# Reading the kept activations and gates back from SyncE's queue instead of ScalarE's

## The chip, the core and the metric

The kernel runs on one core of a Trainium2 chip. The metric is the device time of one execution in microseconds (us). The engines of the core run their own instruction streams and meet only through semaphores: TensorE (PE in the profile, its weight loads PEld), VectorE (DVE), ScalarE (ACT), GpSimd (POOL) and SyncE (SP), which computes nothing and only issues DMAs. DMAs issued by SyncE, ScalarE and GpSimd run in three queues, q1, q10 and q0 of the profile, on the same 16 DMA engines.

## The reference

Two layers of a small transformer over 512 tokens of width 1024. Each layer is a hybrid mixer (attention and a gated recurrence), a layer norm, and a mixture of 16384 one-row experts (`peer_ffn`) whose top 16 per head are picked by product keys. The change lies in the last part:

```python
def block(xb):                       # 128 tokens
    ...                              # top 16 of 16384 experts for each of 8 heads: idx, gate
    act = jax.nn.gelu(jnp.einsum('thkd,td->thk', u[idx], xb).astype(jnp.float32), approximate=False)
    return jnp.einsum('thk,thkd->td', (gate * act).astype(xb.dtype), v[idx])
```

`u` and `v` are 16384 x 1024 in float32 for each layer.

## The kernel before

For the first 128 tokens the kernel gathers the chosen rows of `u` and `v` (GpSimd issues the gathers, VectorE does the sums). For the other 384 tokens it computes densely over all 16384 experts, in 128 tiles of 128 experts. The **first product** multiplies the tokens by every tile of `u`, applies gelu, and stores the activations to `act_dram`; the sparse gates are stored as a dense matrix to `gate_dram`. The **second product** multiplies gate times activation, called `w`, by every tile of `v`, and adds up over all 128 tiles in PSUM.

Every float32 operand is split into a high and a low part (`v_hi`, `v_lo`, `w_hi`, `w_lo`), and each product is three matmuls: high by low, low by high, high by high. For one tile `j` of the second product TensorE runs 6 x 3 = 18 matmuls of 512 columns (`matmul3`, L564), waits for `v_lo` and `w_lo` of that tile before it, and signals `y_done` behind it.

The work around it, with the order that each engine's program has:

- **SyncE** (L511 to L520) loads tile `j` of `v` into one of four places in `panel` as soon as the low part of tile `j - 4` is taken (`need_v_lo(pr, j - TILE_SLOTS)`). It loads nothing else in this stage but two gain vectors at `j == 8`.
- **ScalarE** (L1011 to L1022), in turn `j`: `split_v(j + 3)` (L956: waits for the landing of that tile and for `y_done` of j tiles, and writes `v_hi`), then `split_w(j + 2)` (L973: writes `w_hi`), and in every fourth turn, at `j = 6, 10, ... 114`, `fetch(j // 4 + 3)`: two DMAs (L960, L962) that read the activations and the gates of one panel of four tiles back, 768 KB each. Four panels (`WSLOTS`) have room. `fetch(0)` to `fetch(3)` are issued earlier, the last of them at `j == 2`.
- **VectorE** (L1617 to L1628), in turn `j`: when `j` is a multiple of 4, `weights(j // 4 + 1)` (L1584: activations times gates, waits for both landings); then `low_w(j + 2)` (L1590: waits for `w_hi` of that tile, writes `w_lo`); `low_v(j + 3)` if that is even (L1597: waits for `v_hi`, writes `v_lo`); then `add_row(j - 3)` (L1607, the gathered rows of the first 128 tokens).
- **GpSimd** (L1117 to L1121), in turn `j`: `v_lo` of tile `j + 3` if that is odd (L1111), then the gather of row `j + 3` (L1076, 512 KB).

All waits are in program order: an instruction behind a waiting one on the same engine waits too. A panel may be overwritten when `w_lo` of its four tiles is written, which is what the wait for `w_lo_ready` ahead of the fetch is for.

The loop of ScalarE:

```python
for j in range(NK):
    if j + URING < NK:
        split_v(j + URING)
    if j + 2 < NK:
        split_w(j + 2)
    ...
    if j % GROUP == 2 and j > 2 and j // GROUP + WSLOTS - 1 < UPANELS:
        act.wait_ge(w_lo_ready.sem, layer * w_lo_ready.per_layer + j // GROUP * GROUP)
        fetch(j // GROUP + WSLOTS - 1)
```

Of the kernel before, what the change touches and what calls it, by code (L numbers as in the profile page):

```python
# [23 lines left out]
GROUP = 4  # L24
UPANELS = NK // GROUP
# [12 lines left out]
WSLOTS = 4  # L38
# [24 lines left out]
def build(nc, x, pT, emb_g, emb_b, w_in, fox_fb, fox_g, lbl, hg_g, w_out, ln1_g, ln1_b,  # L63
# [5 lines left out]
    act_dram = nc.dram_tensor("act_scratch", (DEPTH, UPANELS, P, GROUP * DT), F32).ap()  # L69
    gate_dram = nc.dram_tensor("gate_scratch", (DEPTH, BLOCKS, P, NK, TB), F32).ap()  # L70
# [18 lines left out]
    with ExitStack() as ctx:  # L89
# [5 lines left out]
        def sig(name, per_layer, before=0):  # L95
            s = Signal(ctx.enter_context(nc.semaphore(name)), per_layer, before)
            names.append((name, s))
            return s
# [52 lines left out]
        def part(at, *shape):  # L151
            n = 1
            for s in shape:
                n *= s
            ap = arena[:, at:at + n]
            if len(shape) == 2:
                return ap.rearrange("p (a b) -> p a b", b=shape[1])
            if len(shape) == 3:
                return ap.rearrange("p (a b c) -> p a b c", b=shape[1], c=shape[2])
            return ap  # L160
# [36 lines left out]
        def wact(n):  # L197
            return part((20480, 0, 3072, 23552)[n % WSLOTS], GROUP, DT)

        def gin(n):  # L200
            return part((22016, 1536, 4608, 6144)[n % WSLOTS], BLOCKS, GROUP, TB)
# [28 lines left out]
        def u_tile(j):  # L230
            return panel[:, j % 4 // 2, j % 2 * D:(j % 2 + 1) * D]

        def v_tile(j):
            return panel[:, j % 4 // 2, j % 2 * D:(j % 2 + 1) * D]
# [112 lines left out]
        act_in = [sig(f"act_in{r}", 16 * UPANELS // WSLOTS) for r in range(WSLOTS)]  # L347
        gate_in = [sig(f"gate_in{r}", 16 * UPANELS // WSLOTS) for r in range(WSLOTS)]
# [5 lines left out]
        w_lo_ready = sig("w_lo_ready", NK)  # L354
# [50 lines left out]
        def need_v_lo(pr, j):  # L405

            pr.need(v_lo_odd if j % 2 else v_lo_even, j // 2 + 1)
# [38 lines left out]
        @block.sync  # L446
        def _(sp):
            sp.dma_start(h[:], x.rearrange("(i p) d -> p i d", p=P)).then_inc(x_in.sem, 16)
            sp.dma_start(lb_in[:], lbl).then_inc(lb_loaded.sem, 16)
            for k, a in enumerate((emb_g, emb_b)):  # L450
                sp.dma_start(lng[:, k, :], a.partition_broadcast(P)).then_inc(emb_in.sem, 16)
            sp.dma_start(cst[:], consts).then_inc(const_in.sem, 16)
            for layer in range(0, DEPTH):
                pr = Program(sp, layer)
                at = bass.ds(layer, 1)

                def load_panel(k):
                    dst = panel[:, k % 2]
                    if k == 0:

                        src = w_in[at, :, 3 * FW:3 * FW + P].rearrange("l (c p) n -> p (l c) n", p=P)
                        dst = dst[:, 0:NC * P].rearrange("p (c n) -> p c n", n=P)
                    elif k == K_PLE:
                        src = ple_w[at].rearrange("l (c p) n -> p (l c) n", p=P)
                        dst = dst.rearrange("p (c n) -> p c n", n=D)
                    else:
                        j, rows = ((k - 1) // 2, (k - 1) % 2) if k < K_U else ((k - K_GATE) // 2, (k - K_GATE) % 2)
                        w, col = (MIXER_PANELS if k < K_U else GATE_PANELS)[j]
                        src = w[at, rows * KC * P:(rows + 1) * KC * P, col:col + PANEL].rearrange(
                            "l (c p) n -> p (l c) n", p=P)  # L470
                        dst = dst.rearrange("p (c n) -> p c n", n=PANEL)
                    sp.dma_start(dst, src).then_inc(panel_in[k % 2].sem, 16)

                def row(a):
                    return a[at].rearrange("l d -> (l d)").partition_broadcast(P)


                if layer > 0:
                    sp.wait_ge(pled.sem, layer * pled.per_layer)
                    sp.wait_ge(v_lo_even.sem, layer * v_lo_even.per_layer)  # L480
                    sp.wait_ge(v_lo_odd.sem, layer * v_lo_odd.per_layer)
                load_panel(0)

                pr.mark(sp.dma_start(ff_bias[:], fox_fb[at].rearrange("l h -> h l")), ff_in, 16)
                load_panel(1)
                for k, a in enumerate((fox_g, hg_g)):
                    pr.mark(sp.dma_start(ng[:, k, :], row(a)), gains_in, 16)

                sp.wait_ge(h_ready.sem, layer * h_ready.per_layer + h_ready.before)
                for k, a in enumerate((ln1_g, ln1_b)):  # L490
                    pr.mark(sp.dma_start(lng[:, k, :], row(a)), ln1_in, 16)

                sp.wait_ge(dotted.sem, layer * dotted.per_layer)
                pr.mark(sp.dma_start(pTs[:], pT[at].rearrange("l (c p) t -> p (l c) t", p=P)), pT_in, 16)

                for k in range(2, K_PLE + 1):
                    if k == K_U - 6:
                        sp.wait_ge(h_ready.sem, layer * h_ready.per_layer + h_ready.before + NT)
                        pr.mark(sp.dma_start(keys_s, keysT[at].rearrange("l d a n -> d (l a) n")), keys_in, 16)
                    sp.wait_ge(ring_lo_ready.sem, layer * ring_lo_ready.per_layer + 2 + KC * (k - 2))  # L500
                    load_panel(k)

                for j in range(NK):
                    if j < 2:
                        sp.wait_ge(ring_lo_ready.sem, layer * ring_lo_ready.per_layer + SPLITS)
                    elif j < TILE_SLOTS:
                        sp.wait_ge(pled.sem, layer * pled.per_layer + 8)
                    else:
                        sp.wait_ge(u_lo_ready.sem, layer * u_lo_ready.per_layer + j - TILE_SLOTS + 1)
                    pr.mark(sp.dma_start(u_tile(j), u[layer, j]), u_in[j % TILE_SLOTS], 16)  # L510
                for j in range(NK):  # L511
                    if j == 2 * TILE_SLOTS:
                        sp.wait_ge(dotted.sem, layer * dotted.per_layer + SLOTS)
                        for k, a in enumerate((ln2_g, ln2_b)):
                            pr.mark(sp.dma_start(lng[:, k, :], row(a)), ln2_in, 16)
                    if j < TILE_SLOTS:
                        sp.wait_ge(u_lo_ready.sem, layer * u_lo_ready.per_layer + NK - TILE_SLOTS + j + 1)
                    else:
                        need_v_lo(pr, j - TILE_SLOTS)
                    pr.mark(sp.dma_start(v_tile(j), v[layer, j]), v_in[j % TILE_SLOTS], 16)  # L520


# [269 lines left out]
        def _(act):  # L792
# [5 lines left out]
            for layer in range(0, DEPTH):  # L798
                pr = Program(act, layer)
# [44 lines left out]
                for s in range(NS):  # L844
                    n = (s % NT + 1) * P
# [112 lines left out]
                def fetch(n):  # L958

                    pr.mark(act.dma_start(wact(n).rearrange("p g t -> p (g t)"), act_dram[layer, n]),  # L960
                            act_in[n % WSLOTS], 16)
                    pr.mark(act.dma_start(gin(n).rearrange("p j g t -> p j (g t)"),  # L962
                                          gate_dram[layer, :, :, n * GROUP:(n + 1) * GROUP, :]
                                          .rearrange("j p g t -> p j (g t)")), gate_in[n % WSLOTS], 16)
# [46 lines left out]
# [5 lines that stand above are left out]
                    if j == 2:  # L1016
                        act.wait_ge(dotted.sem, layer * dotted.per_layer + SLOTS)
                        pr.mark(nc.scalar.activation(wgt0, act0, ACT.Gelu), gelu0_done)
                        fetch(3)
                    if j % GROUP == 2 and j > 2 and j // GROUP + WSLOTS - 1 < UPANELS:  # L1020
                        act.wait_ge(w_lo_ready.sem, layer * w_lo_ready.per_layer + j // GROUP * GROUP)
                        fetch(j // GROUP + WSLOTS - 1)  # L1022
                root(4, rstd[:])


# [682 lines left out]
```

## Time and profile before

| | us |
|---|---|
| median of 3 runs | 3805.31 (3805.03 to 3805.52) |
| the profiled execution | 3803.14 |
| its span, first to last instruction | 3801.3 |
| TensorE busy | 3493.6 (92%) |
| VectorE busy | 2784.0 (73%) |
| GpSimd busy | 2183.2 (57%) |
| ScalarE busy | 1112.6 (29%) |
| the chain that ended last: matmuls of L564 | 61% of the span |

The second product of layer 0 starts at 1365.8 us of the span, and that of layer 1 ends at 3771.7 us. The stretches 1400 to 1800 us and 3300 to 3700 us lie wholly within the two. Where a group of instructions is busy for longer than the pitch at which its instructions follow each other, they overlap: a matmul of 512 columns is shown with 389 ns, and they start 0.226 us apart.

### The profile page before, as it was taken

How to read it: one execution, taken by the hardware profiler on the slowest of the kernel's cores; microseconds unless marked ns; L12 is line 12 of the kernel's file. 1: busy time of each engine (PE TensorE's matmuls, PEld its weight loads, DVE VectorE, ACT ScalarE, POOL GpSimd, SP SyncE). 2: the span in 40 equal slices, each digit the busy share in tenths (PEclk: the TensorE clock that was granted, in tenths of full speed). 3: DMA queues.
4: the chain of work that ended last, by engine and by line, in shares of the span. 5: the costliest groups of instructions: out<-in, count | busy, mean ns of one | idle time of the engine just before them, and what ended most of it. 6: DMA issues, size and time to landing. Idle time of an engine off the chain costs nothing.

```text
span 3801.3 us, 47667 instructions
## 1 busy us (share of the span) xinstructions
PE 3493.6 (92%) x17690; PEld 3065.9 (81%) x17690; DVE 2784.0 (73%) x5495; ACT 1112.6 (29%) x1748; POOL 2183.2 (57%) x1420
## 2 busy tenths in 40 slices
PE   6997779999989989999889977799999899899996
PEld 5766668899989978888777666679999899788885
DVE  5436636999896569999962374369988965899998
ACT  1112201334333333333221121013333333333332
POOL 5901467677646655555477025568666566555553
PEclk9956889999999999999999578899999999999998
DMA  4300022578868899999732001217888688999995
GB/s 138 98 14 1 12 78 79 187 261 311 295 232 298 301 380 357 353 352 354 258 94 89 1 1 34 78 67 242 275 295 300 229 312 305 370 354 356 353 354 184
DMA packets 316646, 822.01 MB, mean 216 GB/s; under 512 B 22400, under 2 KB 122752, under 8 KB 313088
## 3 DMA queue, kind: packets, MB, share of 16 engines
q1 hardware_dynamic: 112256, 349.15, 26.9%
q0 software_dynamic: 73728, 268.47, 19.1%
q10 hardware_dynamic: 130432, 201.34, 15.1%
q8 instruction: 142, 2.33, 0.2%
q14 instruction: 88, 0.72, 0.1%
HBM read 716.12 MB, written 102.76 MB: 215 GB/s over the span
## 4 chain that ended last, share of the span: by engine, by line
PE 74%; DVE 19%; POOL 2%; issue 2%; DMA 1%; ACT 1%; SPq 0%; ACTq 0%; DVEq 0%; POOLq 0%
PE ps L564 61%; PE ps L773 4%; PE ps L615 2%; DVE work L1467 2%; DVE state L1530 2%; PE ps L636 2%; PE ps L619 1%; DVE work L1471 1%; POOL ring_lo L1042 1%; DVE expert L1473 1%; DVE arena L1521 1%; DVE arena L1330 1%; PE ps L628 1%; POOL ring_hi L1040 1%; DVE arena L1338 1%
## 5 line engine op out<-in xcount | busy, mean ns | idle before, releaser
L1094 POOL TENSOR_TENSOR u_lo<-panel,u_hi 128x1024 fp32r<-128x1024 f32 x256 | 616.3, 2408 | 270.0 <-ACT u_hi L920 268.3
L564 PE MATMUL ps<-hT_hi,u_lo 128*128 128x384 f32 x2048 | 705.6, 345 | 3.9 <-POOL u_lo L1094 3.9
L564 PE MATMUL ps<-hT_lo,u_hi 128*128 128x384 f32 x2048 | 688.1, 336 | 0.0
L564 PE MATMUL ps<-hT_hi,u_hi 128*128 128x384 f32 x2048 | 687.8, 336 | 0.0
L564 PE MATMUL ps<-v_hi,w_lo 128*128 128x512 f32 x1536 | 599.8, 390 | 26.1 <-DVE w_lo L1590 26.1
L564 PE MATMUL ps<-v_lo,w_hi 128*128 128x512 f32 x1536 | 599.2, 390 | 0.0
L564 PE MATMUL ps<-v_hi,w_hi 128*128 128x512 f32 x1536 | 599.0, 390 | 0.0
L1111 POOL TENSOR_TENSOR v_lo<-panel,v_hi 128x1024 fp32r<-128x1024 f32 x128 | 348.5, 2723 | 389.7 <-ACT v_hi L956 381.3
L920 ACT CAST u_hi<-panel 128x1024 fp32r<-128x1024 f32 x256 | 268.1, 1048 | 723.1 <-PE ps L564 706.7
L956 ACT CAST v_hi<-panel 128x1024 fp32r<-128x1024 f32 x256 | 269.5, 1053 | 673.3 <-PE ps L564 665.6
L1590 DVE TENSOR_TENSOR w_lo<-arena,w_hi 128x384 fp32r<-128x384 f32 x256 | 393.9, 1540 | 93.8 <-ACT w_hi L973 93.7
L1040 POOL TENSOR_TENSOR ring_hi<-panel,cst 128x512 fp32r<-128x512 f32 x244 | 273.8, 1122 | 288.4 <-PE ps L564 174.8
L564 PEld LDWEIGHTS ps<-hT_hi,u_lo 128*128 128x128 f32 x2048 | 388.4, 190 | 5.4 <-POOL u_lo L1094 4.9
L564 PEld LDWEIGHTS ps<-hT_lo,u_hi 128*128 128x128 f32 x2048 | 388.1, 190 | 0.5 <-issue 0.5
L564 PEld LDWEIGHTS ps<-hT_hi,u_hi 128*128 128x128 f32 x2048 | 387.0, 189 | 0.0
L564 PEld LDWEIGHTS ps<-v_hi,w_lo 128*128 128x128 f32 x1536 | 289.4, 188 | 87.7 <-issue 27.3
L1042 POOL TENSOR_TENSOR ring_lo<-panel,ring_hi 128x512 fp32r<-128x512 f32 x244 | 336.3, 1378 | 19.1
L564 PEld LDWEIGHTS ps<-v_hi,w_hi 128*128 128x128 f32 x1536 | 289.3, 188 | 60.2
L564 PEld LDWEIGHTS ps<-v_lo,w_hi 128*128 128x128 f32 x1536 | 289.4, 188 | 60.0
L1607 DVE SCALAR_TENSOR_TENSOR ps<-rows_mem,arena,ps 128x1024 f32<-128x1024 f32 x256 | 327.2, 1278 | 0.4
L1067 POOL TENSOR_TENSOR arena<-arena 128x896 f32<-128x896 f32 x32 | 84.4, 2638 | 389.9 <-DVE arena L1338 389.9
L1076 POOL DMA_INDIRECT rows_mem<-in_v_rows,arena x256 | 264.6, 1033 | 58.3 <-issue 44.8
(220 smaller groups left out, 6284.2 us busy)
## 6 DMA issues: line engine op xcount, KB each, us to landing
panel<-in_u SPq DMA_DIRECT2D x256, 512.0 KB, 4.2
panel<-in_v SPq DMA_DIRECT2D x256, 512.0 KB, 6.8
act_scratch<-arena ACTq DMA_DIRECT2D x128, 384.0 KB, 4.1
gate_scratch<-arena ACTq DMA_DIRECT2D x24, 2048.0 KB, 9.3
arena<-act_scratch ACTq DMA_DIRECT2D x64, 768.0 KB, 6.7
arena<-gate_scratch ACTq DMA_DIRECT2D x64, 768.0 KB, 14.3
panel<-in_w_in SPq DMA_DIRECT2D x28, 1024.0 KB, 5.2
panel<-in_wq SPq DMA_DIRECT2D x16, 1024.0 KB, 5.1
```

What stands on the lines that cost most here:

```text
L564: mm = nc.tensor.matmul(o, lhs[a], rhs[b_], start=(start and n == 0), stop=(stop and n == 2))
L773: mm = nc.tensor.matmul(g_bank(k)[:, c * NK:(c + 1) * NK], hot1[:, k % 2, c, :], hot2[:, k % 2, c, :], start=True, stop=True)
L920: pr.mark(nc.scalar.copy(u_hi[:, j % URING].rearrange("p c n -> p (c n)"), u_tile(j)), u_hi_ready)
L956: pr.mark(nc.scalar.copy(v_hi[:, j % VRING], v_tile(j)), v_hi_ready)
L1040: nc.gpsimd.tensor_tensor(r_hi[:, at], src, zeros, ALU.subtract).then_inc(ring_hi_ready.sem, 1)
L1042: nc.gpsimd.tensor_tensor(r_lo[:, at], src, r_hi[:, at].bitcast(F32), ALU.subtract).then_inc(ring_lo_ready.sem, 1)
L1067: pr.mark(nc.gpsimd.tensor_tensor(ke, ke, kT[:, hd:hd + 1, i * P:(i + 1) * P].to_broadcast([P, LEVELS - 1, P]), ALU.mult), lev_mul)
L1076: pr.mark(nc.gpsimd.indirect_dma_start(out=dst, out_offset=None, in_=rows, in_offset=bass.IndirectOffsetOnAxis(ap=idx0[:, s:s + 1], axis=0 ...
L1094: pr.mark(nc.gpsimd.tensor_tensor(u_lo[:, j % URING].rearrange("p c n -> p (c n)"), u_tile(j), u_hi[:, j % URING].rearrange("p c n -> p (c ...
L1111: pr.mark(nc.gpsimd.tensor_tensor(v_lo[:, j % VRING], v_tile(j), v_hi[:, j % VRING].bitcast(F32), ALU.subtract), v_lo_odd)
L1590: pr.mark(nc.vector.tensor_tensor(w_lo[:, j % GROUP], wact(j // GROUP)[:, j % GROUP], w_hi[:, j % GROUP].bitcast(F32), ALU.subtract), w_lo ...
L1607: pr.mark(nc.vector.scalar_tensor_tensor(out=acc0, in0=v_rows_in[s % VBUF], scalar=wgt0[:, s:s + 1], in1=acc0, op0=ALU.mult, op1=ALU.add), ...
```

## The change

The fetches at `j = 6, 10, ... 114` are taken out of ScalarE's program and put into SyncE's loop over the tiles of `v`. At the same `j` numbers, with the same wait for `w_lo_ready`, SyncE issues the two DMAs of the panel directly ahead of the load of tile `j`. The `j` of the two loops is not the same moment: SyncE's `j` is the tile that it loads, ScalarE's `j` the turn in which it splits tile `j + 3`. `fetch(0)` to `fetch(3)` stay where they were.

```diff
@@ SyncE, loop over the tiles of v @@
                     else:
                         need_v_lo(pr, j - TILE_SLOTS)
+                    if j % GROUP == 2 and j > 2 and j // GROUP + WSLOTS - 1 < UPANELS:
+                        n = j // GROUP + WSLOTS - 1
+                        sp.wait_ge(w_lo_ready.sem, layer * w_lo_ready.per_layer + j // GROUP * GROUP)
+                        pr.mark(sp.dma_start(wact(n).rearrange("p g t -> p (g t)"), act_dram[layer, n]),
+                                act_in[n % WSLOTS], 16)
+                        pr.mark(sp.dma_start(gin(n).rearrange("p j g t -> p j (g t)"),
+                                             gate_dram[layer, :, :, n * GROUP:(n + 1) * GROUP, :]
+                                             .rearrange("j p g t -> p j (g t)")), gate_in[n % WSLOTS], 16)
                     pr.mark(sp.dma_start(v_tile(j), v[layer, j]), v_in[j % TILE_SLOTS], 16)
@@ ScalarE, loop of the second product @@
-                    if j % GROUP == 2 and j > 2 and j // GROUP + WSLOTS - 1 < UPANELS:
-                        act.wait_ge(w_lo_ready.sem, layer * w_lo_ready.per_layer + j // GROUP * GROUP)
-                        fetch(j // GROUP + WSLOTS - 1)
```

SyncE's queue at the start of the second product, with - as it was and + as it is now (`in_v` is a tile of `v`, `act_scratch` and `gate_scratch` the kept activations and gates):

```order
 L510 DMA panel<-in_u 128x1024 x128
-L520 DMA panel<-in_v 128x1024 x8
+L528 DMA panel<-in_v 128x1024 x6
+L523 DMA arena<-act_scratch 128x1536
+L525 DMA arena<-gate_scratch 128x12x128
+L528 DMA panel<-in_v 128x1024 x2
 L515 DMA lng<-in_ln_g 128x1024
 L515 DMA lng<-in_ln_b 128x1024
-L520 DMA panel<-in_v 128x1024 x120
+L528 DMA panel<-in_v 128x1024 x2
+L523 DMA arena<-act_scratch 128x1536
+L525 DMA arena<-gate_scratch 128x12x128
```

Ahead of tile 6, and of every fourth tile behind it up to 114, there are now two more DMAs; before, nothing but tiles stood in this queue.

ScalarE before, in the turns behind `fetch(3)` (`CAST v_hi` is `split_v`, `CAST w_hi` is `split_w`); this piece repeats every four turns:

```order
L956 CAST v_hi<-panel 128x1024
L973 CAST w_hi<-arena 128x384
L960 DMA arena<-act_scratch 128x1536
L962 DMA arena<-gate_scratch 128x12x128
L956 CAST v_hi<-panel 128x1024
L973 CAST w_hi<-arena 128x384
```

Now the two DMAs between the splits are gone, and the splits follow each other in the same order as before. The programs of TensorE, VectorE and GpSimd are the same.

## Rows read from the trace of the kernel before

**Rows 1.** Busy time by stretch (windows): engines, PEclk, DMA share, GB/s; both layers.

```profile
1500.00:1600.00 100.00, 100.00 (x443) 82.81 (x442) 91.64 (x68) 35.95 (x50) 58.91 (x37) 1.00 1.00 354
...
sum 800.00, PE 800.00 PEld 662.40 DVE 733.29 ACT 286.98 POOL 470.19; mean PE 100.00 PEld 82.80 DVE 91.66 ACT 35.87 POOL 58.77
```

**Rows 2.** Waits, 1400 to 1800 us: us in total, times, longest.

```profile
ACT v_hi L956 <- PE ps L564: 253.5, 97, 2.9
...
DVE w_lo L1590 <- ACT w_hi L973: 32.5, 47, 1.0
...
ACT v_hi L956 <- DMA panel<-in_v: 2.9, 1, 2.9
```

**Rows 3.** Waits of SyncE's queue in the same stretch.

```profile
SPq L520 <- POOL v_lo L1111: 208.2, 49, 4.8
SPq L520 <- DVE v_lo L1597: 157.1, 49, 4.5
```

**Rows 4.** Timeline of ScalarE: start, duration, work; one fetch and the splits behind.

```profile
1507.61 0.33 ACTq L960 DMA_DIRECT2D arena<-act_scratch  x1
1507.96 0.46 ACTq L962 DMA_DIRECT2D arena<-gate_scratch  x1
...
1511.58 1.05 ACT L956 CAST v_hi<-panel 128x1024 fp32r<-128x1024 f32 x1 [2.62 <-PE ps L564]
1512.54 0.50 ACT L973 CAST w_hi<-arena 128x384 fp32r<-128x384 f32 x1
```

**Rows 5.** Timeline of VectorE, from `low_w` of tile 4m+1 to that of 4m+3.

```profile
1513.08 0.56 DVE L1590 TENSOR_TENSOR w_lo<-arena,w_hi 128x384 fp32r<-128x384 f32 x1 [0.44 <-ACT w_hi L973]
1513.56 1.22 DVE L1597 TENSOR_TENSOR v_lo<-panel,v_hi 128x1024 fp32r<-128x1024 f32 x1
1514.69 1.28 DVE L1607 SCALAR_TENSOR_TENSOR ps<-rows_mem,arena,ps 128x1024 f32<-128x1024 f32 x1
1515.88 1.75 DVE L1584 TENSOR_TENSOR arena<-arena 128x1536 f32<-128x1536 f32 x1
1517.55 2.75 DVE L1590 TENSOR_TENSOR w_lo<-arena,w_hi 128x384 fp32r<-128x384 f32 x1
1520.23 1.28 DVE L1607 SCALAR_TENSOR_TENSOR ps<-rows_mem,arena,ps 128x1024 f32<-128x1024 f32 x1
1521.42 0.61 DVE L1590 TENSOR_TENSOR w_lo<-arena,w_hi 128x384 fp32r<-128x384 f32 x1
```

**Rows 6.** Timeline of GpSimd beside it: two gathers, and the next odd `v_lo`.

```profile
1511.17 1.09 POOL L1076 DMA_INDIRECT rows_mem<-in_v_rows,arena  x1
1512.57 0.94 POOL L1076 DMA_INDIRECT rows_mem<-in_v_rows,arena  x1 [0.30 <-issue]
1516.80 3.09 POOL L1111 TENSOR_TENSOR v_lo<-panel,v_hi 128x1024 fp32r<-128x1024 f32 x1 [3.28 <-ACT v_hi L956]
```

**Rows 7.** DMA, 1400 to 1800 us: queues (packets, MB, share); issues (us to landing).

```profile
q1 hardware_dynamic: 14349, 52.29, 36.4%
q0 software_dynamic: 14112, 51.39, 33.8%
q10 hardware_dynamic: 41617, 38.22, 29.7%
...
panel<-in_v SPq DMA_DIRECT2D x98, 512.0 KB, 6.8
arena<-act_scratch ACTq DMA_DIRECT2D x24, 768.0 KB, 6.6
arena<-gate_scratch ACTq DMA_DIRECT2D x24, 768.0 KB, 14.2
rows_mem<-in_v_rows,arena POOLq DMA_INDIRECT x99, 7.5
```

**Rows 8.** The tile `panel` in that stretch: landings of single tiles.

```profile
DMA to landing us min/median/max: 3.5/6.8/9.4
```

**Rows 9.** Timeline of TensorE: the first matmul of the second product, layer 0.

```profile
1365.83 0.77 PE L564 MATMUL ps<-v_hi,w_lo 128*128 128x512 f32 x1 [11.67 <-DVE w_lo L1590]
```

**Rows 10.** Window behind it: TensorE alone, then PEclk, DMA share, GB/s.

```profile
1370.00:1374.00 4.00, 4.00 (x19) 1.00 1.03 400
```

## The prediction

> **What bounds the kernel now.** I read the busy time by stretch first, to find out which engine is full in the stage that the change touches. In 800 us taken from the two second products TensorE is busy for all 800, at a granted clock of 1.00, and the DMA engines' share is 1.00 too [rows 1]. So TensorE sets the time here, with 443 matmuls in 100 us: 18 x 100 / 443 = 4.06 us for a tile, 16.25 us for a panel of four. VectorE is next with 91.7%, ScalarE far behind with 35.9%.
>
> Then the waits, to see what is late. ScalarE's `split_v` waits for TensorE in 97 of 98 turns, 253.5 us of 400, and once in 400 us for a tile of `v` to land, 2.9 us [rows 2]. SyncE waits 365 us of 400, always for the low part of a tile, thus for a free place [rows 3]. No row of TensorE is among the waits of this stretch. The reader is to see from this that tiles of `v` are early, that nothing can be gained in the steady part (a full TensorE can't be fuller), and that the question is only whether the change makes something late.
>
> **What it removes.** ScalarE issues two DMAs less for each panel, 0.33 + 0.46 us [rows 4], 28 times in each layer. ScalarE waits for TensorE during most of its time [rows 2], so this is worth 0.
>
> **What it adds.** SyncE issues them. Its time for that, 0.79 us of 16.25, fits its waiting [rows 3]. The panels arrive earlier, which helps nobody: VectorE's `weights` waits for no landing in the steady part, its only wait there is for `w_hi` [rows 2]. Two other things are added to the way of tile 4m+2 of `v`, which now stands behind the fetch. First, SyncE waits until `w_lo` of tile 4m-1 is written. Second, 1.57 MB stand ahead of the tile in the same queue.
>
> **First look: is the tile still in time?** I follow one panel. `w_lo` of tile 4m-1 is the last of rows 5, written at 1521.42 + 0.61 = 1522.03. `split_v` of tile 4m+2 is the row at 1511.58 [rows 4], thus due again at 1511.58 + 16.25 = 1527.83. From the release to the due time there are 5.8 us. Call the time from release to landing Λ.
>
> The trace has no tile behind a fetch in one queue, so I bound Λ. A tile by itself lands after 3.5 us at the least [rows 8]. The fetch ahead of it takes the DMA engines, at the best rate that a stretch shows, 400 GB/s [rows 10], 1.573 / 0.400 = 3.9 us; by the share of its queue, 29.7% of 400 us for 24 pairs [rows 7], 4.9 us. The row gathers of GpSimd's queue run between: 33.8% of 400 us for 99 rows, 1.4 us each, or 1.3 at 400 GB/s. With none of them in the way Λ is 3.5 + 3.9 = 7.4 to 8.4 us. With two of them it is 7.4 + 2.6 = 10.0 to 8.4 + 2.8 = 11.2. Far above these there is another row: gates land 14.2 us after their issue now [rows 7], and with the issue ahead, 0.35, and a tile behind, 1.5 (36.4% of 400 us for 98 tiles), that makes 16.1. I take two gathers and the middle, 10.6, because GpSimd issues its gathers in pairs behind an odd `v_lo` [rows 6] and such a pair is in flight at that moment (worked out below). I don't take 16.1, since today the gates share the engines with tiles of a second queue, which would now stand behind them.
>
> So every value of Λ is above 5.8, and the tile comes late, by 4.8 us with my value. TensorE bears about 3.5 us of this: `w_lo` of tile 4m+2 is written at 1517.55 + 2.75 = 1520.30 [rows 5], and needed three tiles after 1511.58, at 1523.8.
>
> **Second look: the lateness feeds itself.** ScalarE's order is `split_v(4m+2)`, then `split_w(4m+1)`, then VectorE's `low_w(4m+1)`. The w row starts 1513.08 - 1511.58 = 1.5 us behind the start of the v split [rows 4, 5]. From there VectorE works without a gap through seven instructions to the end of `low_w(4m+3)`, 1522.03 - 1513.08 = 8.95 us [rows 5]. That end is the release of the **next** fetch, behind which the next tile 4m+6 stands. So there is now a closed ring of work: tile lands, 1.5 + 8.95 = 10.45 us, release, Λ, next tile lands. It must go round once in four tiles, and it takes 10.45 + 10.6 = 21.05 us, where TensorE needs 16.25. TensorE gets 4.8 us idle in each panel.
>
> Bounds of the first part: one of the seven, the `w_lo` of 2.75 us, is stretched while GpSimd's `v_lo` runs beside it (1516.80, 3.09 us [rows 6]); the same operation takes 0.56 and 0.61 in the other rows [rows 5]. If the late timing moves the two apart, 10.45 becomes 8.3. I keep 10.45, because in the ring an odd tile lands right behind the even one, and GpSimd again works while VectorE does these seven. On the pair of gathers: with the tile landing at 0, TensorE starts tile 4m+1 at 2.1 and ends it at 6.1, then `v_hi` of the next odd tile (1.05), `v_lo` on GpSimd (2.4 to 3.1), and the gathers at about 10 and 11.4 [rows 4, 6], beside a release at 10.45. Both are in Λ.
>
> **The sum.** 28 fetches in each layer, two layers: 56 x 4.8 = 269 us. The first of each layer has no ring behind it, but comes when the DMA engines are over-full (share 1.03 [rows 10]); I count it like the others. Profiled execution 3803.14 + 269 = 4072, and the median of the runs lies 2 us above that execution: **4070 us**. TensorE's granted clock may fall after its new gaps, as it was low for the first matmul behind an idle time of 11.67 us (0.77 us [rows 9] against 0.39); I add nothing, since TensorE isn't in the ring.
>
> **A rule against this reading.** The traces show act data landing after 6.6 us and gates of the same size, issued 0.35 us later in the same queue, after 14.2, while tiles in another queue land in 6.8 [rows 7]: it matters what stands ahead in one's own queue. The Trainium skill, "DMA: Bandwidth & Descriptors", section "Issuing engines are not separate DMA queues", says that DMAs of all issuing engines run on the same 16 DMA engines and interleave, and that the choice of the issuing engine saves only sequencer time; read by itself this gives a change worth nothing. The same page's section "Queues, rings and completion order" says that each DMA engine goes round between queues and takes the descriptors of one queue in their order; by that the tile waits for the whole fetch.
>
> **Rivals.**
>
> 1. *The ring is short enough (not slower).* Place: the landing of tile 4m+2. If Λ is at most 16.25 - 8.3 = 8.0 us together with the short VectorE part, the ring fits under TensorE and the cost is 0: 3803 to 3805 us. For it: the low ends, 7.4 and 8.3, sum to 15.7. Against it: both must hold at once, with no gather in the way, when the DMA share is 1.00 [rows 1]. This is also what the rule on issuing engines would give. Chance 0.05.
> 2. *A small ring*, 16.4 to 18 us, when the gathers miss the fetch or GpSimd misses VectorE: 56 x up to 1.75 = up to 98 us, 3810 to 3900. Chance 0.06.
> 3. *The gates hold the tile for as long as they take now*, Λ = 16.1: 10.45 + 16.1 = 26.5, 56 x 10.3 = 577 us, 4380. For it: 14.2 is measured. Against it: while TensorE idles, the same 16 us of DMA work are spread over 21 and more. Chance of anything above 4180: 0.07.
> 4. *Faster.* ScalarE's queue is free at the start of the stage. But TensorE is busy for 4.00 of 4.00 us right behind its start [rows 10], and its idle 11.67 us [rows 9] wait for `fetch(0)` and its `w`, which aren't moved. Chance 0.02.
> 5. *The change doesn't do what it says*: the order of SyncE's queue shows that it does. 0.
>
> **How the numbers follow.** The ring at 18 to 23 us has 0.80. 18 us give 3803 + 98 = 3900; 23 us, my value with 2 us more for the slowest of the 16 DMA engines, give 3803 + 378 = 4180. The range is 3900 to 4180; what is left out is 0.20. A measurement of this kernel can tell about 0.2% from no change, 8 us. Faster 0.02, within 0.05, slower 0.93 (0.80 + 0.06 + 0.07).
>
> **What would show it.** In the changed kernel's windows of the second product: TensorE busy near 16.25 / 21 = 77%, VectorE near 71%, DMA share below 0.9. In the waits: `split_v` waits for the landing of `panel` about once in each panel, and TensorE for `w_lo`. In SyncE's waits: one for `w_lo` of L1590 in each panel. The fetches are about 21 us apart. Wrong would be: fetches 16.3 us apart with TensorE at 100% (rival 1), or TensorE's waits on something that is not behind tile 4m+2. The first product must be as it was.

## The result: 4199.9 us against 3805.4, slower by 10.4%

The changed kernel takes 4199.89 us (median of 4 executions, 4195.92 to 4208.58), the kernel before, beside it, 3805.41 us. The ratio is 1.104 with a 95% interval of 1.102 to 1.106. The forecast was 4070 with a range of 3900 to 4180: the direction and the mechanism came out, the size did not, and the time lies above the range.

The profile after: its span is 4206.7 us. The windows of the second product of layer 0, five of them from 1400 to 1900 us, with the columns of rows 1:

```profile
1500.00:1600.00 100.00, 79.88 (x309) 63.85 (x308) 55.47 (x46) 22.84 (x32) 45.40 (x27) 0.86 0.70 246
1600.00:1700.00 100.00, 77.59 (x305) 61.45 (x303) 53.59 (x44) 22.88 (x33) 42.43 (x24) 0.88 0.72 256
...
sum 500.00, PE 399.11 PEld 318.06 DVE 288.29 ACT 122.56 POOL 232.85; mean PE 79.82 PEld 63.61 DVE 57.66 ACT 24.51 POOL 46.57
```

TensorE fell from 100 to 80%, with 305 matmuls in 100 us instead of 443 [rows 1], and the DMA engines from 1.00 to 0.70. Nothing is full any more: VectorE has 58% and the DMA engines 70%. When every engine gets emptier and the time grows, the work has been put in a row that was side by side.

The waits between 1500 and 1900 us, and below them those of SyncE's queue, answer rows 2 and 3:

```profile
ACT v_hi L964 <- DMA panel<-in_v: 232.8, 23, 17.0
...
DVE w_lo L1595 <- ACT w_hi L981: 171.5, 17, 12.7
...
PE ps L572 <- DVE w_lo L1595: 81.4, 19, 7.4
ACT v_hi L964 <- PE ps L572: 68.5, 17, 5.5
```

```profile
SPq L522 <- DVE w_lo L1595: 277.0, 17, 18.0
```

`split_v` waited 253.5 us for TensorE and 2.9 for a tile [rows 2]; now it waits 68.5 us for TensorE and 232.8 for tiles. SyncE waited only for free places [rows 3]; now it waits for `w_lo`, 17 times, once for each panel, 16.3 us each.

The chain of waits in the stretch 1620 to 1650 us (start, duration, what) goes once round the ring:

```profile
1617.89 11.08 DMA panel<-in_v
...
1629.94 0.52 ACT w_hi L981
...
1630.96 1.22 DVE v_lo L1602
1632.18 0.92 DVE ps L1612
...
1636.64 0.55 DVE w_lo L1595
1637.19 1.20 DVE ps L1612
1638.39 3.26 DVE w_lo L1595
...
1641.71 0.33 SPq L523
...
1642.08 0.61 SPq L525
...
1642.74 11.00 DMA panel<-in_v
```

There is no TensorE in it. A tile lands, ScalarE and VectorE work from `w_hi` of tile 4m+1 to `w_lo` of tile 4m+3, SyncE issues the fetch, and the next tile lands 11 us behind its own issue. The page's section on the whole chain says the same in shares:

```profile
PE 45%; DVE 24%; DMA 18%; issue 7%; POOL 2%; ACT 2%; SPq 1%; ACTq 0%; DVEq 0%; POOLq 0%
PE ps L572 34%; DMA panel<-in_v 17%; PE ps L781 4%; DVE ps L1612 3%; PE ps L623 2%; DVE work L1472 2%; DVE w_lo L1595 2%; DVE state L1535 2%; PE ps L644 1%; DVE v_lo L1602 1%; DVE work L1476 1%; PE ps L627 1%; POOL ring_lo L1047 1%; DVE expert L1478 1%; DVE arena L1526 1%
```

The fetches are 23.6 us apart (the mean of the 54 intervals in both layers, from the issues in SyncE's timeline; the first of each layer is 29.7 or 29.8 us, the others are 23.4 in the mean), instead of 16.3. 56 x (23.6 - 16.3) = 409 us; the spans differ by 405.

Of two fetches that follow each other, here is SyncE's timeline, and what it issues behind them:

```profile
1617.05 0.33 SPq L523 DMA_DIRECT2D arena<-act_scratch  x1
1617.41 0.44 SPq L525 DMA_DIRECT2D arena<-gate_scratch  x1
1617.89 5.78 SPq L528 DMA_DIRECT2D panel<-in_v  x4
1641.71 0.33 SPq L523 DMA_DIRECT2D arena<-act_scratch  x1
```

And ScalarE's, at the landing between them:

```profile
1628.99 1.04 ACT L964 CAST v_hi<-panel 128x1024 fp32r<-128x1024 f32 x1 [10.32 <-DMA panel<-in_v]
1629.94 0.51 ACT L981 CAST w_hi<-arena 128x384 fp32r<-128x384 f32 x1
```

From the issue at 1617.05 to the landing at 1628.99 are 11.9 us, one of the shortest of the ring's DMA parts; over the 56 fetches the mean is 14.0 us, from 11.9 to 17.5. The other part, landing to next issue, is 9.6 us in the mean, and here, at 12.7, one of the longest.

### The profile page after: what moved, and what is told of

Read it like the earlier page. It is cut to its first block, busy times and chain, and to the rows that moved or that the text cites. A ratio compares the mean times of both kernels' runs of the same rounds, so it can differ in the third digit from the quotient of the medians.

```text
span 4206.7 us, 47723 instructions
## 1 busy us (share of the span) xinstructions
PE 3621.3 (86%) x17690; PEld 3139.9 (75%) x17690; DVE 2687.2 (64%) x5495; ACT 1103.9 (26%) x1748; POOL 2250.1 (53%) x1420
## 4 chain that ended last, share of the span: by engine, by line
PE 45%; DVE 24%; DMA 18%; issue 7%; POOL 2%; ACT 2%; SPq 1%; ACTq 0%; DVEq 0%; POOLq 0%
PE ps L572 34%; DMA panel<-in_v 17%; PE ps L781 4%; DVE ps L1612 3%; PE ps L623 2%; DVE work L1472 2%; DVE w_lo L1595 2%; DVE state L1535 2%; PE ps L644 1%; DVE v_lo L1602 1%; DVE work L1476 1%; PE ps L627 1%; POOL ring_lo L1047 1%; DVE expert L1478 1%; DVE arena L1526 1%
## 5 line engine op out<-in xcount | busy, mean ns | idle before, releaser
L572 PE MATMUL ps<-v_hi,w_lo 128*128 128x512 f32 x1536 | 654.9, 426 | 299.3 <-DVE w_lo L1595 298.8
L572 PE MATMUL ps<-v_lo,w_hi 128*128 128x512 f32 x1536 | 641.9, 418 | 0.0
L572 PE MATMUL ps<-v_hi,w_hi 128*128 128x512 f32 x1536 | 639.0, 416 | 0.0
L572 PEld LDWEIGHTS ps<-v_hi,w_lo 128*128 128x128 f32 x1536 | 318.3, 207 | 395.6 <-issue 326.4
L1595 DVE TENSOR_TENSOR w_lo<-arena,w_hi 128x384 fp32r<-128x384 f32 x256 | 221.5, 866 | 598.7 <-ACT w_hi L981 598.6
L572 PEld LDWEIGHTS ps<-v_hi,w_hi 128*128 128x128 f32 x1536 | 314.8, 205 | 71.7
L572 PEld LDWEIGHTS ps<-v_lo,w_hi 128*128 128x128 f32 x1536 | 318.1, 207 | 67.1
L1081 POOL DMA_INDIRECT rows_mem<-in_v_rows,arena x256 | 332.3, 1298 | 66.6 <-issue 42.2
```

Source lines behind the costliest of these rows:

```text
L572: mm = nc.tensor.matmul(o, lhs[a], rhs[b_], start=(start and n == 0), stop=(stop and n == 2))
L1081: pr.mark(nc.gpsimd.indirect_dma_start(out=dst, out_offset=None, in_=rows, in_offset=bass.IndirectOffsetOnAxis(ap=idx0[:, s:s + 1], axis=0 ...
L1595: pr.mark(nc.vector.tensor_tensor(w_lo[:, j % GROUP], wact(j // GROUP)[:, j % GROUP], w_hi[:, j % GROUP].bitcast(F32), ALU.subtract), w_lo ...
```

## Experiments

The text behind "expected" was written before each run. There are 14 kernels. The kernel before, run beside them, had a median of 3803.8 us (kernels e1 to e4), 3804.5 (e5, e6, e7, e9) and 3805.7 (e8, e10 to e12), and in one execution beside the last two 3814.6. Where no ratio is given, there is one execution of the kernel; e3, e9 and f1 leave out 120 of the 128 gathers of `v` in each layer, and f2 the gates that it doesn't read. I call **Λ** the time from the end of `low_w` of tile 4m+3 to the landing of the next tile 4m+2 (the start of its `split_v`, which waited for it), and **D** the time from there to the end of the next such `low_w`; both are read from the timelines of VectorE and ScalarE between 1500 and 1900 us, 16 to 20 panels each. Where no view shows the landing of a single tile, it is read from the updates of that tile's semaphore in the trace.

| kernel | us | Λ | D | ring |
|---|---|---|---|---|
| changed | 4199.9 | 13.6 | 9.7 | 23.3 |
| wait alone | 4051.2 | 9.6 | 11.5 | 21.1 |
| activations only | 4074.2 | 11.1 | 10.3 | 21.3 |
| changed, long pieces | 4127.2 | 12.6 | 9.7 | 22.2 |
| changed, no gathers | 4018.6 | 9.7 | 10.1 | 19.8 |

### e1: the wait alone

```diff
# kernel before, SyncE's loop; the fetches stay on ScalarE
+ if j % GROUP == 2 and j > 2 and j // GROUP + WSLOTS - 1 < UPANELS:
+     sp.wait_ge(w_lo_ready.sem, layer * w_lo_ready.per_layer + j // GROUP * GROUP)
  pr.mark(sp.dma_start(v_tile(j), v[layer, j]), v_in[j % TILE_SLOTS], 16)
```

> The fetches stay on ScalarE as in the kernel before; SyncE only gets the wait for w_lo of tile 4m-1 ahead of tile 4m+2. Ring theory: the ring is closed, 9.5 us (tile landed to release, as the changed kernel shows) plus the landing of a tile that stands behind nothing, 3.5 to 6.8 us, so 13 to 16.3 us in all, against 16.25 us of TensorE: 0 to 50 us over the kernel before, 3805 to 3855. Rival, the wait alone is the cause (the tile comes too late whatever stands ahead of it): about the whole loss, 4150 to 4200.

Measured: 4051.24 us, ratio 1.0655 (1.0633 to 1.0678). Neither text had it right. The wait alone makes 247 of the 395 us, with not one byte added to SyncE's queue. Its windows and SyncE's waits:

```profile
1600.00:1700.00 100.00, 85.31 (x344) 66.99 (x343) 68.95 (x52) 26.07 (x37) 46.47 (x28) 0.95 0.79 286
```

```profile
SPq L521 <- DVE w_lo L1592: 329.1, 19, 19.9
```

The ring is there with 21.1 us. I had expected 3.5 to 6.8 us for a tile with nothing ahead in its queue; it is 9.6. The other queues' work stands around the release: in this trace ScalarE issues a fetch 1.3 to 5.0 us ahead of the held tile, and GpSimd a gather 3.7 to 3.9 us and another 0.3 or 1.1 us ahead of it (1500 to 1900 us). That the gathers lengthen Λ is shown by e9 below; the part of this fetch in it was not taken apart.

### e2: the bytes without the wait

```diff
# changed kernel, SyncE's loop: the same fetch, one panel later in the program
- if j % GROUP == 2 and j > 2 and j // GROUP + WSLOTS - 1 < UPANELS:
-     n = j // GROUP + WSLOTS - 1
-     sp.wait_ge(w_lo_ready.sem, layer * w_lo_ready.per_layer + j // GROUP * GROUP)
+ if j % GROUP == 2 and j // GROUP > 1 and j // GROUP + WSLOTS - 2 < UPANELS:
+     n = j // GROUP + WSLOTS - 2
+     sp.wait_ge(w_lo_ready.sem, layer * w_lo_ready.per_layer + (j // GROUP - 1) * GROUP)
```

> The fetches stand ahead of tiles 4m+2 in SyncE's queue as in the changed kernel, but each one panel later in the program (ahead of tile 4m+6 instead of 4m+2), so its wait for w_lo is long fulfilled: the bytes ahead of the tile without the wait. Ring theory: the only ring left goes through v_lo of the tile four before, 3.2 us plus 12 to 14 us to the landing, 15.2 to 17.2 us against 16.25: 0 to 55 us over the kernel before, 3805 to 3860. Rival, the 1.57 MB ahead in the same queue are the cause by themselves: the loss stays mostly, 4100 to 4200.

Measured: 3810.78 us, ratio 1.0017 (1.0007 to 1.0027), near the low end of the ring theory's text, and far from the rival's 4100 to 4200. The same 1.57 MB stand ahead of every tile 4m+2, and cost 7 us in all. SyncE's timeline shows the pace of TensorE, and the tile `panel` the landings of all tiles, 11.3 us behind the issue at the most:

```profile
1602.53 0.33 SPq L523 DMA_DIRECT2D arena<-act_scratch  x1
1602.90 0.43 SPq L525 DMA_DIRECT2D arena<-gate_scratch  x1
1603.38 12.34 SPq L528 DMA_DIRECT2D panel<-in_v  x4
1618.85 0.33 SPq L523 DMA_DIRECT2D arena<-act_scratch  x1
```

```profile
DMA to landing us min/median/max: 3.5/7.5/11.3
```

So the bytes ahead of the tile are not a cause by themselves. They lengthen a ring, and cost time only where one is closed. From the issue of the fetch to the landing of tile 4m+2 are 10.7 us here in the mean (10.0 to 12.1 between 1500 and 1875 us), where the changed kernel has 13.5 in the same stretch.

### e3: what is in Λ, the gathers

```diff
# changed kernel, GpSimd: only the first 8 gathers of v; VectorE waits only for those
+ if s < VBUF:
      gather(v_rows, v_rows_in[s % VBUF], s, v_row_in[s % VBUF])
```

> The changed kernel without 120 of the 128 row gathers of v in each layer (the sums over the gathered rows then use old rows; this part of the computation is left out). It measures what the gathers have in the 14 us from release to landing. Ring theory with three to four gathers of 1.3 to 1.4 us in them: 14 falls to 8.5 to 10, the ring to 18 to 19.5 us, 3900 to 3990. If the prediction's two gathers were right and something else is slow: 11 to 11.5 us, ring near 20.7, 4050. If the gathers have no part in it: 14 us stay, 4190.

Measured: 4018.57 us. Λ falls from 13.6 to 9.7, by 3.9 us, which is nearly three gathers of 1.4 us [rows 7]. Λ hit the first text, the time missed it by 29 us, since D is 10.1 and not 9.5. The prediction had two gathers in it. The removal also takes their issue out of GpSimd's program, so 3.9 us is what the gathers do in all, and not the DMA time of three of them by measurement.

### e5 and f2: what is in Λ, the fetch, half of it, and its pieces

```diff
# changed kernel: the gates go back to ScalarE at j % 4 == 2, the activations stay on SyncE
- pr.mark(sp.dma_start(gin(n)..., gate_dram[layer, :, :, n * GROUP:(n + 1) * GROUP, :]...), gate_in[n % WSLOTS], 16)
+ pr.mark(act.dma_start(gin(n)..., gate_dram[layer, :, :, n * GROUP:(n + 1) * GROUP, :]...), gate_in[n % WSLOTS], 16)
```

> As the changed kernel, but only the activations (0.79 MB) are read back on SyncE's queue, ahead of tile 4m+2 and behind the wait; the gates stay on ScalarE at their old place. If bytes ahead of the tile lengthen the ring in proportion, half of the step from the wait alone (4051) to the whole change (4200) is left: 4110 to 4150. If the gates with their 1536 pieces of 512 B are the slow part: 4050 to 4080. If any fetch ahead of the tile costs the same: 4180 to 4200.

Measured: 4074.24 us, one execution. Λ is 1.5 us above that of the wait alone, D 1.2 us below. All three kernels read the same bytes; what differs is the queue in which they stand. A byte is not a byte here, since the gates, as many, add 2.5 us more when they too go ahead of the tile.

```diff
# changed kernel: the second DMA of the fetch reads 768 KB in rows of 6 KB
- gate_dram[layer, :, :, n * GROUP:(n + 1) * GROUP, :].rearrange("j p g t -> p j (g t)")
+ act_dram[layer, n]
```

> The changed kernel, but the second DMA of each fetch on SyncE's queue reads the 768 KB of the activations once more instead of the gates: the same bytes at the same place of the queue, without the source's pieces of 512 B (the product of gate and activation is thus not computed there). Measured so far: act alone ahead of the tile adds 1.5 us to the landing, act and gates 4.6. If a byte is a byte: 14.2 us stay within 0.7, 4170 to 4200. If the pieces of 512 B are dear: 14.2 falls to 12.6, twice the step of the activations, 4100 to 4130.

Measured: 4127.23 us. Λ is 12.6, 1.0 us less with the same bytes. So of the gates' 2.5 us some 1.0 is due to their pieces of 512 B, and 1.5 to their bytes, as with the activations.

### e4: the tile first

```diff
# changed kernel, SyncE's loop at j % 4 == 2
  sp.wait_ge(w_lo_ready.sem, layer * w_lo_ready.per_layer + j // GROUP * GROUP)
+ pr.mark(sp.dma_start(v_tile(j), v[layer, j]), v_in[j % TILE_SLOTS], 16)
  pr.mark(sp.dma_start(wact(n)..., act_dram[layer, n]), act_in[n % WSLOTS], 16)
  pr.mark(sp.dma_start(gin(n)..., gate_dram[...]), gate_in[n % WSLOTS], 16)
- pr.mark(sp.dma_start(v_tile(j), v[layer, j]), v_in[j % TILE_SLOTS], 16)
```

> The changed kernel with tile 4m+2 issued directly ahead of the fetch instead of behind it; the wait stays ahead of both. Ring theory: tile 4m+2 now lands 4 to 7 us behind the release, and the ring goes through tile 4m+3, which stands behind the fetch: from its landing 1.5 us to w_hi, then low_w(4m+2), add_row, low_w(4m+3), 2.3 to 4.6 us, then 12 to 14 us to the next landing, 16 to 20 us, middle 18: 3805 to 4015, middle 3905. Rival, all bytes of the queue count wherever they stand: no change, 4190.

Measured: 4128.15 us. A gain of 72 us over the changed kernel, far less than expected: tile 4m+2 lands 7.9 us behind the release (mean of the panels between 1500 and 1900 us), but the release itself waits longer, since tile 4m+3 is now the late one and `low_w(4m+2)` and `low_w(4m+3)` need it. The ring has 22.1 us. To order the queue otherwise gave back only 72 of the 395 us while all of it stood behind one release.

### e6: one instruction earlier

```diff
# kernel with the wait alone
- sp.wait_ge(w_lo_ready.sem, layer * w_lo_ready.per_layer + j // GROUP * GROUP)
+ sp.wait_ge(w_lo_ready.sem, layer * w_lo_ready.per_layer + j // GROUP * GROUP - 1)
```

> As the kernel with the wait alone (fetches on ScalarE), but SyncE waits for w_lo of tile 4m-2 instead of 4m-1, one instruction of each kind earlier in VectorE's program. Ring theory: the VectorE part of the ring gets 1.75 us shorter (add_row and low_w), so the ring of 20.7 us goes to about 19, 3803 + 56 x 2.7 = 3950, 3930 to 3970. If the mere presence of a wait ahead of the tile costs (not when it is fulfilled): 4050 as with the full wait. If there is a threshold in the timing and not a ring: 3805.

Measured: 3801.62 us. Waiting for `w_lo` of tile 4m-2 instead of 4m-1 takes away the whole loss. SyncE still waits for `w_lo` once a panel:

```profile
SPq L521 <- DVE w_lo L1592: 178.7, 20, 8.9
SPq L522 <- POOL v_lo L1113: 98.8, 25, 4.8
```

but its rings no longer set the pace: the tiles 4m+2 from 14 to 114 of layer 0 land 3.5 to 6.4 us behind their issue, 3.8 in the median, and at least 1.2 us before `split_v` takes them.

The time fits the third text, the one against the ring. The ring can still be added up, but only with a Λ from this kernel: from the landing to the end of `low_w(4m+2)` are 1520.30 - 1511.58 = 8.7 us [rows 4, 5], and 8.7 + 3.8 = 12.5 us, 15.1 with the largest, is less than 16.3. My 19 us were wrong because I took Λ over from the slow kernel. The one instruction of each kind by itself doesn't close the ring either: 10.45 + 3.8 = 14.3 us. Λ must grow as well, and it does, as the first held tile of e10 below shows: 7.5 us. What differs around the two issues is GpSimd's pair of gathers. Here the second of them comes behind the tile, there both stand ahead of it (SyncE's and GpSimd's timelines, e6 and then e10; L1078 is a gather, and x2 the held tile and the next):

```profile
1619.19 1.09 POOL L1078 DMA_INDIRECT rows_mem<-in_v_rows,arena  x1 [0.15 <-issue]
1619.53 0.81 SPq L522 DMA_DIRECT2D panel<-in_v  x2
1620.59 0.94 POOL L1078 DMA_INDIRECT rows_mem<-in_v_rows,arena  x1 [0.30 <-issue]
```

```profile
1445.38 1.09 POOL L1078 DMA_INDIRECT rows_mem<-in_v_rows,arena  x1 [0.15 <-issue]
1446.77 0.94 POOL L1078 DMA_INDIRECT rows_mem<-in_v_rows,arena  x1 [0.30 <-issue]
1447.46 0.81 SPq L522 DMA_DIRECT2D panel<-in_v  x2
```

### e10, e11, e12, e9: where the ring starts, and whether it holds itself

```diff
# kernel with the wait alone (e10)
- if j % GROUP == 2 and j > 2 and j // GROUP + WSLOTS - 1 < UPANELS:
+ if j % GROUP == 2 and j >= 22 and j // GROUP + WSLOTS - 1 < UPANELS:
# kernel e6 (e11), kernel before (e12): ahead of the load of tile j
+ if j == 30:
+     sp.wait_ge(y_done.sem, layer * y_done.per_layer + 28)
```

> The kernel with the wait alone, but the wait begins at tile 22 instead of tile 6, when the stage runs at TensorE's pace. There, release to due is 5.9 us, a tile with no fetch ahead landed in 4.0 to 7.1 us where the stage kept its pace, and TensorE bears 3.5 us. If there are two states, one at TensorE's pace (16.3 us) and one in which the late tile also gathers all other DMA work behind the release (21 us), and the full start of the stage throws the kernel into the slow one, this one stays at the pace: 3800 to 3815. If the wait itself makes the ring of 20.7 us wherever it begins: 24 panels x 2 x 4.4 = 210 us, 4000 to 4030.

Measured: 3999.46 us. The same wait, begun only at tile 22, costs 48 panels x 4.0 us. So the start of the stage isn't what sets the ring off. This kernel shows the onset. ScalarE's `split_v` of the tiles 18, 22, 26 and 30 (start, duration, and in brackets what it waited for):

```profile
1436.93 1.05 ACT L958 CAST v_hi<-panel 128x1024 fp32r<-128x1024 f32 x1 [2.61 <-PE ps L566]
...
1454.82 1.05 ACT L958 CAST v_hi<-panel 128x1024 fp32r<-128x1024 f32 x1 [4.19 <-DMA panel<-in_v]
...
1473.82 1.05 ACT L958 CAST v_hi<-panel 128x1024 fp32r<-128x1024 f32 x1 [6.87 <-DMA panel<-in_v]
...
1491.76 1.05 ACT L958 CAST v_hi<-panel 128x1024 fp32r<-128x1024 f32 x1 [8.49 <-DMA panel<-in_v]
```

Tile 18, not yet held, is in time, 16.3 us behind tile 14 like all before it. Tile 22, the first that is held, lands 7.5 us behind its release (the `w_lo` that ended at 1447.36) and is 1.6 us late at once. Tiles 26 and 30 land 8.9 and 8.7 us behind theirs, and D keeps its 9.3 to 10.4: the ring takes 17.9, then 19.0, then 17.9 us. Between 1500 and 1900 us Λ is 9.1 us in the mean (7.5 to 10.1).

> The kernel that waits for one w_lo less (3802 us, at TensorE's pace), with one disturbance in each layer: tile 30 of v is held back until TensorE has done tile 27. With two states the single late tile throws it into the slow ring of some 19 us for the rest of the stage: 22 panels x 2 x 2.5 = 110 us, 3880 to 3940. With one state it recovers: 3805 to 3820.

Measured: 3816.50 us. One tile held back in each layer does not throw the kernel with the shorter wait into the slow ring; it recovers. In layer 0 the `split_v` of tile 34 comes 13.1 us behind that of the late tile 30, the next 15.5 us behind, and from tile 42 on they are 16.3 us apart again.

> Control: the kernel before with the same single late tile 30 in each layer. No wait of SyncE for w_lo, so no ring through it: only the disturbance itself, 3 to 6 us in each layer: 3808 to 3820 in either theory.

Measured: 3819.30 us; the disturbance itself costs as much. So no run shows two states of one kernel. With the shorter wait the ring is under TensorE's 16.3 us and late tiles catch up; with the full wait it is over it and they don't, as long as tiles are held.

The gathers decide this too. The kernel with the full wait alone, without 120 of 128 gathers:

> The kernel with the wait alone, without 120 of the 128 row gathers of v in each layer (that part of the computation is left out). Theory of the burst: what stands in the way of tile 4m+2 there is the work of the other two queues, which now comes at the same moment: three gathers (4.1 us, as their removal showed in the changed kernel) and part of a fetch. Ring 20.7 - 3 to 4.1 = 16.6 to 17.7: 3825 to 3885. If the landing is slow for another reason: 4000 to 4050.

Measured: 3806.71 us, less than expected. Without gathers the held tiles 4m+2 from 18 to 114 of layer 0 land 3.3 to 3.8 us behind their issue, the ring needs 10.4 + 3.5 = 13.9 us, and the kernel keeps TensorE's pace. The release and the fetch behind it stand here as at tile 22 of e10 (ScalarE's fetch comes 1.9 us behind the tile, there 1.8); only the gathers are gone, and the tile lands after 3.5 us instead of 7.3 (7.5 from the release). The gathers around the release are what takes Λ over the limit there.

### e7 and f1: the fetch three tiles later

```diff
# changed kernel, SyncE's loop: the fetch of the same panel, ahead of tile 4m+5
- if j % GROUP == 2 and j > 2 and j // GROUP + WSLOTS - 1 < UPANELS:
-     n = j // GROUP + WSLOTS - 1
-     sp.wait_ge(w_lo_ready.sem, layer * w_lo_ready.per_layer + j // GROUP * GROUP)
+ if j % GROUP == 1 and j > 5 and j // GROUP + WSLOTS - 2 < UPANELS:
+     n = j // GROUP + WSLOTS - 2
+     sp.wait_ge(w_lo_ready.sem, layer * w_lo_ready.per_layer + (j // GROUP - 1) * GROUP)
```

> The fetches on SyncE's queue with the wait of the changed kernel for the same panel, but ahead of tile 4m+5 instead of 4m+2, by when the wait is fulfilled anyway. Ring theory: no instruction of SyncE waits for w_lo any more; what is left is the tile behind 1.57 MB, with a ring over the odd v_lo of 3.6 + 12 to 13 us, at or just under 16.25: 3803 to 3820. Rival, any fetch in the tiles' queue costs: over 3900.

Measured: 3944.29 us, ratio 1.0363 (1.0336 to 1.0389). Expected was next to nothing. No instruction of SyncE waits for `w_lo` here; its waits show another ring, over GpSimd's `v_lo` of the odd tile:

```profile
SPq L528 <- DVE v_lo L1602: 200.0, 42, 5.3
SPq L523 <- POOL v_lo L1116: 135.3, 21, 7.9
```

GpSimd's timeline tells why its DMA part is long. Behind the `v_lo` that releases the fetch (issued at 1616.04) it issues two gathers at once, and soon two more:

```profile
1613.66 2.35 POOL L1116 TENSOR_TENSOR v_lo<-panel,v_hi 128x1024 fp32r<-128x1024 f32 x1 [8.31 <-ACT v_hi L964]
1616.17 1.09 POOL L1081 DMA_INDIRECT rows_mem<-in_v_rows,arena  x1 [0.15 <-issue]
1617.56 0.94 POOL L1081 DMA_INDIRECT rows_mem<-in_v_rows,arena  x1 [0.30 <-issue]
```

The tile behind the fetch lands at 1631.75, 15.7 us later (15.4 in the mean, against 10.7 in e2 with the same bytes ahead), and 3.5 + 15.7 = 19.2 us is above 16.3.

> The kernel with the fetches ahead of tile 4m+5 (3944 us), without 120 of the 128 row gathers of v in each layer (that part of the computation is left out). Its ring goes over GpSimd: landing of tile 4m+5 to the end of its v_lo 3.5 us, then 15.7 us to the next landing, 19.2 in all, and GpSimd issues two gathers right behind the same v_lo and two more behind the next. If those gathers are what makes its landing later than in the kernel with the fetch a panel later (at most 12 us), 15.7 falls by four times 1.4 to 10, the ring to 13.7, below TensorE's 16.3: 3800 to 3812. If the place behind the fetch is the reason by itself: above 3880.

Measured: 3809.68 us. Without the gathers this ring is gone as well: the same landing takes 9.3 us in the mean. The place behind the fetch is dear only with the gathers of the same moment in it.

### e8: looking for a faster version

```diff
# kernel before, ScalarE at the start of the second product
  fetch(1)
- fetch(2)
  ...
  for j in range(2):
      split_w(j)
+ fetch(2)
```

> The kernel before with one change: ScalarE issues fetch(2) behind split_w(0) and split_w(1) instead of ahead of them. At the start of the stage ScalarE was held by the issue of that fetch for 6.3 us, and its first w_hi came at 1364.6 us, 4 us after weights(0) had ended at 1360.6; TensorE waited for it. If that wait is the last one there: 4 us in each layer, 3796 to 3800. If the first landings of v or v_lo are as late, or fetch(2) now comes later for weights(2): no change, 3803 to 3806.

Measured: 3807.62 us, ratio 1.0009 (1.0000 to 1.0018). No gain. The first `w_hi` came 1.7 us earlier, but TensorE still waited for `w_lo`:

```profile
1368.52 0.77 PE L564 MATMUL ps<-v_hi,w_lo 128*128 128x512 f32 x1 [14.02 <-DVE w_lo L1590]
```

It started at 1368.52, later than the 1365.83 of rows 9. In the two traces VectorE had become the last one: it came to that `w_lo` at 1366.12 without a wait, where it had waited 1.10 us for `w_hi` before and started at 1365.13. Its `weights(0)` began later too, at 1361.04 instead of 1358.86, behind the sums over the gathered rows of `u`. How much of that comes from one execution to the next wasn't settled. None of the kernels beats the kernel before by more than its measurement can tell.

## Why the prediction was right about the cause and wrong about the size

- **What bounds, what is gained: right.** TensorE was full, and nothing was gained.
- **First look, the tile comes late: right.** Every value that was given for Λ was above 5.8 us. The onset of e10 is that step as it happened, with the milder kernel.
- **The ring: right.** It is the chain of the changed kernel, link by link. Its VectorE part was put at 10.45 us and measured 9.6 to 9.7. What it lost is the contention that the prediction named: the `w_lo` of 2.75 us [rows 5] took 0.55 in some panels, as at 1636.64, while `weights` (3.44 instead of 1.75) or another `w_lo` (3.33) bore it instead.
- **Λ: wrong, and this is the term that missed.** 10.6 us were taken, 13.6 to 14.0 measured (the second from the issue of the fetch). At TensorE's pace the value would have done: e2 has 10.7 us for the same load behind the same fetch. The step that failed was to size Λ from rows of a kernel at that pace and to carry it into the closed ring, where the gathers stand closer around the release: they start 3.7 and 1.1 us ahead of the fetch's issue and 3.4 and 4.8 us behind it in most panels, in e2 3.7 and 2.3 us ahead and 5.2 and 6.6 behind. That this spacing makes the whole of the 3 us was not tested by itself. Two gathers were counted, the removal of all took 3.9 us, nearly three; the fetch was counted by its bytes, 3.9 to 4.9 us, but its pieces of 512 B cost 1.0 us beyond them. The middle of the bounds left out both, and the bound of 11.2 was no bound, since it was made of the same two gathers. The ring of 23.3 to 23.6 us is above the 23 us at which the range ended; the 2 us that the range had on top for the slowest DMA engine come from no row, and no run shows such a term. 3 us too little in Λ are 56 x 3 = 168 us, 0.8 us too much in D take 45 back, and 4070 + 168 - 45 = 4193.
- **The 16.1 us** from today's landing of the gates were set aside with two reasons, that the gates share the engines with tiles of another queue today, and that TensorE would idle and spread the DMA work. The engines did get free time (0.70), but gathers, fetch and tiles still stood together around the release, and a share over a stretch says nothing of that moment. The measured 14.0 us lie nearer to 16.1 than to 10.6, so 0.07 for all times above 4180 was too little.
- **Rival 1**, that the change costs nothing. The same bytes in the same queue a panel later cost 0.17% (e2). The Trainium skill, "DMA: Bandwidth & Descriptors", section "Issuing engines are not separate DMA queues", says that the choice of the issuing engine saves only sequencer time; e2 agrees with that. The whole change measured 10.4%, and there the measurement decides: 247 of the 395 us come with the wait alone, and the other 148 come with the bytes' place in a ring that is closed.
- **Not foreseen:** that the wait alone makes 247 us of the 395. The prediction charged the ring with the fetch as its main part; the ring closes without it.
- **The windows** were to show TensorE at 77%, VectorE at 71% and the DMA below 0.9. Measured 80, 58 and 0.70. TensorE is above 16.3 / 23.4 = 70%, and its granted clock is down to 0.86 to 0.88, so the same matmuls took longer (416 to 426 ns in the mean over the execution against 389 at full clock). VectorE is below 15.0 / 23.4 = 64%, since fewer of its instructions are stretched beside GpSimd: its `w_lo` took 0.86 us in the mean from 1500 to 1900 us, 1.59 before. TensorE is not in the ring, and what VectorE does in it is D.
- **Open:** without gathers Λ is still 9.7 us, where a tile alone (3.5), act and gates (1.5 + 1.5 + 1.0 as measured) make 7.5. The last 2 us are not accounted for.

## What to carry to other kernels

Before an instruction is put into a queue with a wait of its own, write down what is behind it in that queue and follow that to the wait: if it comes back to the same wait, add up the ring, and compare it with the time that the bounding engine takes for as many tiles. Size the DMA part of such a ring by all the work that stands in every queue around the same release, not by an average share, and don't carry its value from one timing over to another; here one instruction more or less in the ring decided between 0 and 250 us. Of the places tried for this fetch, the one where its wait had long been fulfilled cost 7 us; but e7, whose wait was fulfilled too, lost 140 us through another ring, so the place has to be checked against every ring that passes it.

## What the runs showed of the hardware

- The same 512 KB load (tile 4m+2, held tiles from 1500 to 1900 us) landed 3.5 to 6.4 us behind its issue in the kernel that waits for one `w_lo` less, and 8.5 to 12.1 us in the one with the full wait, where gathers and a fetch stand ahead of it, though the DMA engines' share from 1500 to 1900 us was lower there (0.77 against 0.92). Without the gathers it took 3.3 to 3.8 us with the full wait.
- 768 KB that went ahead of a load in its own queue lengthened that load's Λ by 2.5 us when they were read in pieces of 512 B from the source, and by 1.5 us in rows of 6 KB (one execution each).
- What a GpSimd operation costs VectorE beside it, 1.7 to 2.8 us here, is paid by whichever VectorE operation between SBUF tiles is running: `w_lo` (0.55 to 3.33 us), `v_lo` (1.21 to 3.92) or `weights` (1.75 to 3.44). The `add_row`, which adds onto PSUM, kept its 1.28 us beside it too (30 times in the changed kernel, 19 in e1).
